# Softmax weights scaled in place, turned plainly, and routing moved beside the out-projection

## The reference, cut to what matters

```
def sink_softmax(s, sink):            # s: (..., queries, keys)
    col = broadcast(sink)             # one more column, dropped after
    return softmax(concat([col, s], -1), -1)[..., 1:]
...
p = sink_softmax(concat([s_loc, s_ctx], -1), sink)
o = einsum(p[..., :span], v) + einsum(p[..., span:], v_ctx)
...
g_val, g_idx = top_k(g_logit, 1)      # group
e_val, e_idx = top_k(e_logit[group], 2)
gates = p_group * softmax(e_val)
```

## Time and profile before

| | |
|---|---|
| median of 3 runs | 3037.66 us (3034.0 to 3044.69) |
| the profiled execution | 3045.0 us, span 3043.2 us |
| PE busy in the span | 2741.7 us (90%) |
| DVE, ACT, POOL busy | 1069.0, 459.5, 316.7 us |
| mean granted clock of TensorE | 0.945 of full speed |
| data read from HBM | 743.04 MB |
| attention, layers 0 and 1 | 1278 to 1386, 2232 to 2322 us |
| out-projection, layers 0 and 1 | 1386 to 1478, 2323 to 2382 us |
| routing to the first expert product | to 1530, to 2428 us |
| experts' loops | to about 2072, to about 2997 us |

### The profile page before, as it was taken

One profiled execution on the slowest core, in us unless ns is written; L12 is line 12 of the kernel. 1 busy time (PEld: TensorE's weight loads), 2 busy tenths in 40 slices (PEclk: granted clock), 3 DMA queues, 4 the chain that ended last, 5 costly groups with the idle time before them and its releaser, 6 DMA issues.

```text
span 3043.2 us, 33073 instructions
## 1 busy us (share of the span) xinstructions
PE 2741.7 (90%) x11436; PEld 1249.1 (41%) x11436; DVE 1069.0 (35%) x2093; ACT 459.5 (15%) x874; POOL 316.7 (10%) x445
## 2 busy tenths in 40 slices
PE   7999999999998999999689898986999699999863
PEld 3444444444444446565433232322555433333321
DVE  4999960320003032364631111115544521111104
ACT  3111121100101010451101000002142100101000
POOL 0101112000000000000122111110000121122110
PEclk9999999999998999999799999997989699999986
DMA  6656341212220211001579999995201699999983
GB/s 226 218 189 198 111 181 57 100 56 82 83 83 1 94 56 56 28 1 71 207 284 393 395 393 393 391 341 223 100 1 51 222 358 394 385 347 337 361 326 134
DMA packets 272217, 603.12 MB, mean 198 GB/s; under 512 B 18436, under 2 KB 43332, under 8 KB 272000
## 3 DMA queue, kind: packets, MB, share of 16 engines
q1 hardware_dynamic: 256864, 580.70, 52.2%
q0 software_dynamic: 15264, 21.24, 2.0%
HBM read 743.04 MB, written 29.20 MB: 254 GB/s over the span
## 4 chain that ended last, share of the span: by engine, by line
PE 74%; SPq 10%; DMA 7%; DVE 5%; issue 2%; ACT 2%; POOL 0%; POOLq 0%; DVEq 0%; ACTq 0%
PE psum L1408 13%; PE psum L1020 11%; PE psum L1107 11%; PE psum L1242 9%; SPq L655 9%; PE psum L1078 7%; DMA arena<-in_w 5%; PE psum L1430 5%; PE psum L1346 5%; PE psum L1289 3%; PE psum L1278 2%; PE psum L1005 1%; PE psum L1128 1%; PE psum L1395 1%; PE psum L1301 1%
## 5 line engine op out<-in xcount | busy, mean ns | idle before, releaser
L1408 PE MATMUL psum<-arena 128*64 128x512 f32 x2656 | 639.5, 626 | 89.0 <-DMA arena<-in_w 87.3
L1408 PEld LDWEIGHTS psum<-arena 128*64 128x64 f32 x2656 | 191.9, 143 | 415.9 <-issue 410.7
L1020 PE MATMUL psum<-arena 128*128 128x512 f32 x768 | 341.2, 600 | 2.6 <-ACTq L752 2.6
L1107 PE MATMUL psum<-arena 128*128 128x512 f32 x768 | 329.9, 593 | 0.8 <-ACT arena L731 0.8
L1430 PE MATMUL psum<-arena 128*64 128x512 f32 x1328 | 303.1, 600 | 0.8 <-issue 0.8
L1507 DVE SCALAR_TENSOR_TENSOR arena<-arena 128x512 f32<-128x512 f32 x451 | 300.1, 745 | 0.0
L1242 PE MATMUL psum<-arena 128*128 128x512 f32 (+1 forms) x800 | 288.4, 520 | 5.4 <-ACT arena L818 5.4
L1078 PE MATMUL psum<-arena 128*128 128x512 f32 x512 | 224.4, 602 | 5.2 <-POOL arena L2205 4.4
L1107 PEld LDWEIGHTS psum<-arena 128*128 128x128 f32 x768 | 146.1, 190 | 184.0 <-issue 183.0
L1020 PEld LDWEIGHTS psum<-arena 128*128 128x128 f32 x768 | 143.7, 191 | 176.9 <-issue 174.0
L1242 PEld LDWEIGHTS psum<-arena 128*128 128x128 f32 x800 | 151.7, 192 | 128.8 <-issue 113.4
(11 more groups left out here) (294 smaller groups left out, 2055.1 us busy)
## 6 DMA issues: line engine op xcount, KB each, us to landing
arena<-in_w SPq DMA_DIRECT2D x261, 2048.0 KB, 19.0
arena<-in_w_ada SPq DMA_DIRECT2D x48, 1024.0 KB, 5.2
arena<-in_conv_w_in SPq DMA_DIRECT2D x24, 1024.0 KB
arena<-in_ret_w_in SPq DMA_DIRECT2D x12, 2048.0 KB, 7.9
arena<-in_w_in SPq DMA_DIRECT2D x8, 2048.0 KB, 9.3
arena<-moe_out SPq DMA_DIRECT2D x10, 1024.0 KB, 10.2
arena<-in_conv_w_out SPq DMA_DIRECT2D x4, 2048.0 KB, 11.9
arena<-in_ret_w_out SPq DMA_DIRECT2D x4, 2048.0 KB, 7.8
```

Source lines behind the costliest of these rows:

```text
L1020: m = pe.matmul(bank(b + c), w[:, k, c * P:(c + 1) * P], c_hT[:, k, :], start=(k == 0), stop=(k == KD - 1))
L1107: m = pe.matmul(bank(4 * (n % 2) + j), l_, r_, start=(k == 0), stop=(k == KD - 1))
L1408: m = pe.matmul(bank(2 * s)[part], m_xsT[s][:, at:at + SB], m_w[s][j][:, k, :], start=(k == 0), stop=(k == KD - 1))
```

## The change

In the attention the diagonals are gone. `weights` multiplies the exponentials themselves, in place in `b_sb` (128 rows by 256, 512 or 640 keys per head), by the reciprocal, and `turn` is a plain transpose against the identity. `sink_shift`, `sink_exp` and `weights` are split in two halves of four heads; on DVE the first half of `weights(i+1)` stands after the chunk before the last of tile i, the second after its last.

In the out-projection, from the third tile on, PE turns tile t-1 between the two halves of product t, and the logits of tile t-1 follow product t directly (before: t-2). On DVE the copy and the rows of tile i-1 stand between the two half sums of tile i. The routing operations become a function `route(t0, t1)`, called after the norm of tile i for the tiles whose logits are due (tiles 0 and 1 together, then one each), and once more for the last two tiles where the whole routing stood.

```diff
 def turn(i, c, kv):
...
-                        m = pe.matmul(bank(4 + kv, P, hh * P), b_sb[i % 2][:, 4 * kv + hh, c * P:(c + 1) * P],
-                                      b_dg[i % 2][:, 4 * kv + hh, :], start=True, stop=True)
+                        m = pe.transpose(bank(4 + kv, P, hh * P), b_sb[i % 2][:, 4 * kv + hh, c * P:(c + 1) * P], ident)
...
                     for hf in range(2):
+                        if hf == 1 and t >= 2:
+                            mod_transposes(2 * l + 1, t - 1)
...
-                    if t >= 1:
-                        mod_transposes(2 * l + 1, t - 1)
+                    if t == 1:
+                        mod_transposes(2 * l + 1, 0)
+                    if t == 2:
+                        pe.wait_ge(sem("wr"), past("wr", l) + 16)
+                        logits(0)
                     if t >= 2:
-                        pe.wait_ge(sem("wr"), past("wr", l) + 16)
-                        logits(t - 2)
-                logits(nt - 2)
+                        logits(t - 1)
                 mod_transposes(2 * l + 1, nt - 1)
                 logits(nt - 1)
...
                 for i_ in range(nt):
-                    stats_of(i_)
                     if free:
+                        first(i_, tiles[i_], 0)
                         if i_ >= 1:
                             mod_copy(mod_q, i_ - 1)
-                        norm(i_)
                         if 1 <= i_ < nt - 1:
                             rows(i_ - 1)
+                        first(i_, tiles[i_], 1)
+                        stats_of(i_)
+                        norm(i_)
+                        if 2 <= i_ < nt - 1:
+                            route(i_ - 1 if i_ > 2 else 0, i_)
                         continue
...
+                def weights(i, half):
+
+                    o = 100 + 40 * (i % 2) + 4 * half
+                    W = P * len(att_keys(queries[i]))
+                    rs, esk, rinv = (stats[:, o + 8 * j:o + 8 * j + 4] for j in (2, 3, 4))
+                    dve.wait_ge(sem("at_e"), past("at_e", l) + (AH + 2) * i + 5 * (half + 1))
                     link(dve.tensor_tensor(rs, rs, esk, ALU.add))
                     link(dve.reciprocal(rinv, rs))
-                    for h in range(AH):
-                        dve.tensor_scalar(b_dg[i % 2][:, h, :], ident, rinv[:, h:h + 1], None, ALU.mult)\
-                            .then_inc(sem("at_p"), 1)
+                    for hh in range(4):
+                        p = b_sb[i % 2][:, 4 * half + hh, 0:W]
+                        dve.tensor_scalar(p, p, rinv[:, hh:hh + 1], None, ALU.mult).then_inc(sem("at_p"), 1)
...
-                        if more and nk > 2 and c in (1, 2):
-                            masked(i + 1, c + 1)
-                        if more and c == min(nk, 3) - 1:
-                            sink_shift(i + 1)
-                        if more and c == min(nk, 4) - 1:
-                            weights(i + 1)
+                            sink_shift(i + 1, c)
+                        elif more and c == 1:
+                            sink_shift(i + 1, 0)
+                            masked(i + 1, 2)
+                        elif more and c == 2:
+                            masked(i + 1, 3)
+                            sink_shift(i + 1, 1)
+                        if more and c == max(nk - 2, 0):
+                            weights(i + 1, 0)
+                        if more and c == nk - 1:
+                            weights(i + 1, 1)
...
+                def route(t0, t1):
+
+                    n, r = t1 - t0, slice(t0, t1)
+                    dve.wait_ge(sem("lg_mm"), past("lg_mm", l) + t1)
...
+                finish_rows(2 * l, tiles, add_product, 2 * l + 1,
+                            lambda: dve.wait_ge(sem("ob_mm"), past("ob_mm", l) + 2 * nt), route)
+                route(nt - 2, nt)
```

More of the change, by code:

```diff
@@ L907, in attended @@
                                            o[:, :, h_, :], ACT.Copy).then_inc(sem("at_o"), 1)
-                for pair in range(4):
-                    exps(0, pair)
-                sink_exp(0)
+                for half in range(2):
+                    exps(0, 2 * half)
+                    exps(0, 2 * half + 1)
+                    sink_exp(0, half)
                 mixed_copied(nt - 1)
@@ L924, in _ @@
                             exps(i + 1, 2 * c + 1)
-                        if more and c == min(nk, 4) - 1:
-                            sink_exp(i + 1)
+                            sink_exp(i + 1, c)
+                        elif more and c in (1, 3):
+                            sink_exp(i + 1, c // 2)
                 attended(nt - 1)
@@ L1653, in _, with finish_rows @@
             r_gate(RH - 1)
-            def finish_rows(q, tiles, first, mod_q, free=None):
+            def finish_rows(q, tiles, first, mod_q, free=None, route=None):
                 nt = len(tiles)
                 def stats_of(i_):
-                    first(i_, tiles[i_])
                     for hf in range(2):
@@ L1897, in _ @@
                 masked(0, 3)
-                sink_shift(0)
-                weights(0)
+                sink_shift(0, 1)
+                weights(0, 0)
+                weights(0, 1)
                 for i in range(nt):
@@ L1966, in _, with first_of @@
                 iota = mem(TAB + T_I, 120)
-                def first_of(dst, idx, vals, top, width):
-                    it = iota[:, 0:width].unsqueeze(1).to_broadcast([P, nt, width])
-                    link(dve.tensor_tensor(dst, vals, over(top, nt, width), ALU.is_equal))
+                def first_of(dst, idx, vals, top, n, width):
+                    it = iota[:, 0:width].unsqueeze(1).to_broadcast([P, n, width])
+                    link(dve.tensor_tensor(dst, vals, over(top, n, width), ALU.is_equal))
@@ L1979, in _ @@
-                link(dve.tensor_reduce(gmax, lg[:, :, 0:NG], AX.X, ALU.max))
-                dve.tensor_tensor(ge, lg[:, :, 0:NG], over(gmax, nt, NG), ALU.subtract).then_inc(sem("rt_dve"), 1)
-                first_of(goh, gi, lg[:, :, 0:NG], gmax, NG)
-                link(dve.tensor_scalar(gc, goh, -1.0, BIG, ALU.add, ALU.mult))
-                for t in range(nt):
-                    link(dve.tensor_tensor(el[:, t, :].rearrange("p (g e) -> p g e", g=NG),
-                                           lg[:, t, NG:NG + E].rearrange("p (g e) -> p g e", g=NG),
-                                           gc[:, t, :].unsqueeze(2).to_broadcast([P, NG, EPG]), ALU.add))
@@ L1996, in _ @@
[L1996 to L1997 removed]
+                    link(dve.tensor_tensor(dst, dst, over(idx, n, width), ALU.is_equal))
+                def route(t0, t1):
+                    n, r = t1 - t0, slice(t0, t1)
+                    dve.wait_ge(sem("lg_mm"), past("lg_mm", l) + t1)
+                    rb = mem(SMALL + V_RB + (NG + E) * l, NG + E).unsqueeze(1).to_broadcast([P, n, NG + E])
+                    logit = bank(6, (NG + E) * n, (NG + E) * t0).rearrange("p (t e) -> p t e", t=n)
+                    group = lg[:, r, 0:NG]
+                    link(dve.tensor_tensor(lg[:, r, :], logit, rb, ALU.add))
+                    link(dve.tensor_reduce(gmax[:, r], group, AX.X, ALU.max))
+                    last_ge = dve.tensor_tensor(ge[:, r, :], group, over(gmax[:, r], n, NG), ALU.subtract)
+                    if t1 == nt:
+                        last_ge.then_inc(sem("rt_dve"), 1)
+                    first_of(goh[:, r, :], gi[:, r], group, gmax[:, r], n, NG)
+                    link(dve.tensor_scalar(gc[:, r, :], goh[:, r, :], -1.0, BIG, ALU.add, ALU.mult))
+                    for t in range(t0, t1):
+                        link(dve.tensor_tensor(el[:, t, :].rearrange("p (g e) -> p g e", g=NG),
+                                               lg[:, t, NG:NG + E].rearrange("p (g e) -> p g e", g=NG),
+                                               gc[:, t, :].unsqueeze(2).to_broadcast([P, NG, EPG]), ALU.add))
+                    link(dve.tensor_reduce(m1[:, r], el[:, r, :], AX.X, ALU.max))
+                    first_of(oh1[:, r, :], i1[:, r], el[:, r, :], m1[:, r], n, E)
+                    link(dve.scalar_tensor_tensor(out=el[:, r, :], in0=oh1[:, r, :], scalar=-3 * BIG, in1=el[:, r, :],
+                                                  op0=ALU.mult, op1=ALU.add))
+                    link(dve.tensor_reduce(m2[:, r], el[:, r, :], AX.X, ALU.max))
+                    first_of(oh2[:, r, :], i2[:, r], el[:, r, :], m2[:, r], n, E)
+                    last_ed = dve.tensor_tensor(ed[:, r], m2[:, r], m1[:, r], ALU.subtract)
+                    if t1 == nt:
+                        last_ed.then_inc(sem("rt_dve"), 1)
+                    link(dve.tensor_tensor(M[:, r, :], oh1[:, r, :], oh2[:, r, :], ALU.add))
+                    if t0 == 0:
+                        link(dve.memset(before[:, 0, :], 0.0))
+                    for t in range(t0, min(t1, nt - 1)):
+                        link(dve.tensor_tensor(before[:, t + 1, :], before[:, t, :], M[:, t, :], ALU.add))
```

65 lines of the change are left out of this document (23 added, 42 removed).

## The result

The changed kernel took 3022.8 us in the median of 7 runs (3021.3 to 3027.6), the kernel before 3042.6 beside it (3034.0 to 3044.7). The ratio is 0.9948 (95% interval 0.9934 to 0.9961): 12 to 20 us faster, where 34.5 were forecast and 3003 us with them. Its profiled execution has a span of 3019.9 us, that of the kernel before 3043.2.

A forecast was written before the change was run, and what follows sets the result against it. PE bounds the attention (busy 98.9 of 108 and 83.4 of 90 us); DVE has room. Attention 34, less 4 for the clock, plus 4.5 from the tails: 34.5 us off the median of 3037.66 gives 3003, range 2989 to 3020.

The forecast's parts named there:

- The larger one, plus 0.7 for the hand-over: Attention tile: larger of PE's 14.9 and DVE's 15.5 us, plus 0.7, makes 16.2 instead of 20.7, a gain of 4.5.
- The rival of growing hand-overs: Attention: DVE becomes the limit and its hand-overs grow; gain 15 us in all, 3023 us, chance 0.18.
- its price of 0.72 for the scaling: Attention on DVE: scaling 640 elements in place costs 0.72 us instead of 0.55, a tile 1.4 us more.
- The turn at 0.44 us: Attention on PE: a plain-transpose call takes 0.44 us instead of 0.99, saving at least 0.55 on each of 80 calls.
- Clock, 4 us: Attention on PE: two more half-clock stretches of 7 us, each costing about 2 us, 4 us taken off.
- Nothing of PE waits: Out-projection: routing on DVE fits beside the products and transposes between halves get their norm in time; cost nothing.
- The tail: After the last out-projection product: 2.6 us of steps move ahead, gather issued 5.6 us earlier in layer 0, 3.9 in layer 1.
- The gather, 2.5 us given back: First expert gather in each layer: runs beside the first experts' weights on the DMA engines, giving back 2.5 us.
- +4.5: Out-projection tails of both layers after the gather's loss: 3.1 and 1.4 us left, 4.5 in all, bounds 0 and 9.5.
- The range: Whole kernel: measured time expected between 2989 and 3020 us.
- transposes between halves with an idle time ahead of them: Out-projection on PE: listed among the signs that would show the forecast wrong; no size given.
- rival A: Attention: DVE becomes the limit, hand-overs grow; gain 15 us, 3023 us, chance 0.18; sign: scaling 640 elements well over 0.55 us.

The follow-up runs named there:

- comb1: Changed kernel; ACT makes four- and five-key tiles' last second copy, two-key tiles scale next first half later, tile 0's logits between halves: 3003.2 us, ratio 0.9890.
- w_late: Changed kernel with the scaling of the next tile's first half moved behind the last chunk's copy on DVE: one run, 3008.3 us.
- act_copy: Changed kernel with the second copy of a tile's last chunk moved from DVE to ACT: 3013.3 us, ratio 0.9916.
- no_scale: Changed kernel without the scaling of the weights, so softmax isn't normalised: tiles 81.4 and 59.5 us, whole time not comparable.
- comb2: comb1, but four- and five-key tiles scale the next tile's first half between third chunk's copy and last masked scores: 3000.5 us, ratio 0.9884.
- sp_hold: Changed kernel with the second expert stream's first weights requested only after the first gather has landed: one run, 3039.2 us.
- route_only: Kernel before with only the out-projection and routing edits, attention as before: 3039.4 us, ratio 1.0006.
- tr3: Changed kernel with tile 1's transposes kept behind tile 2's product, between halves only from tile 3's product on: one run, 3018.3 us.

## Why the prediction was wrong

With two profiles of each kernel the account closes. Means, before less after: tiles 7.2 us in layer 0 and 9.3 in layer 1; first out-product to first expert product +0.2 and -3.2; the last loop 2.1; starts, loop of layer 0 and what lies ahead -1.1. Sum 14.5, against 15.8 by the ratio. That PE bounded the attention and that the change is faster by more than 0.3% was right; the size was not. (The 3003 us also stood on a median of 3037.66 for the kernel before, which was 3042.6 beside the change; that alone would have made it 3008.)

- **"The larger one, plus 0.7 for the hand-over"**: the step that failed. The time that it gave can be had: the tile takes 16.48 us in comb1 for 16.2, and start and tiles together 87.6 for the 108.2 of before where 18.2 less were forecast, 75.9 for 90.4 where 15.7 less were. But an engine is only as busy as its sum if the work that others wait for isn't behind work that nobody needs yet. DVE scaled the next tile ahead of the copy that PE's last values wait for, and it waited for ACT ahead of masked scores. The tiles got 7.2 and 9.3 us. That this order costs PE its time is shown in layer 0 by w_late, where nothing but the order changed; in layer 1 w_late gave 1.6 us, all of it clock, and more is shown only together with the copy moved to ACT (act_copy, comb1). The rival of growing hand-overs (15 us in all, 3023, chance 0.18) had this place and the time nearly right, though not its price of 0.72 for the scaling: that was 0.55.
- **The turn at 0.44 us**: mis-sized. It became 0.51 a call in pairs and 0.59 alone; the ten of the tile went from 10.11 to 5.45 us, so a call saves 0.47, not 0.55. With the scores, which grew beside it, PE's sum of the tile is 16.4 in no_scale, not 14.9. The forecast had the limit on DVE (15.5 to 14.9); measured, PE's sum is the larger (16.2 to 13.9 in comb1), so that the 16.2 us of the tile came so near is luck in part. I had taken the lowest price at hand for calls that alternate with scores and values.
- **Clock, 4 us**: too small. No row showed a stretch of 7 us that costs 2; those seen behind waits last some 3.4 us and cost 1.2 to 1.7. With the same instructions and the same form of both starts, PE is busy over the tiles 78.3 and 58.0 us in after and 72.8 and 56.0 in comb2: 7.5 us. It comes with DVE's waits, not with the transposes: a clock of 0.92 and 0.93 in after, 0.98 and 0.95 in comb2.
- **"Nothing of PE waits" in the out-projection**: failed at tile 1. I took the norm's 4.3 us from the tail, where nothing stands ahead of it (it took 4.8 there). In the loop DVE's queue has the copy of tile 0 (1.36) and its scaled rows (1.21) ahead of the second half sum, and that sum took 2.42 beside POOL: the norm was done at 1416.0, 9.8 us behind the product's end at 1406.2. And tile 1 has no logits behind it, so it was due at 7.8. Without the 1.7 us lost beside POOL some 0.3 of the wait of 2.0 would be left (an estimate from these rows); neither delay was tested apart.
- **The tail**: right in layer 0. From the last product to the rank matmul pass 18.85 us (1476.55 to 1495.40); forecast were 27.1 less 2.6 and 5.6, 18.9. But that product ended 98.0 us into the stage instead of the forecast 94.1, by the wait and the half clock: of 5.6 us earlier, 1.75 were left; in layer 1 of 3.9, 0.6: there the wait took 2.0, and the tail 19.7 us for a forecast of 18.7, with the last transposes at half clock (1.97 us for 1.09).
- **The gather, 2.5 us given back**: right, from the gather to its reader 3.72 us became 5.74 in layer 0 and 2.6 became 5.6 in layer 1, with the DMA engines busy 0.26 of the first stretch and 0.89 of the second in layer 0, and sp_hold shows its cause. With so little won ahead of it, it turned the routing half into a loss of 3 us up to the experts in layer 1, which a last loop 2.1 us shorter nearly covered: +4.5 became about 0 (route_only).
- **The range** ended at 3020; the median was 3 us beyond. It rested on sums of busy time, not on the order of the queues.

The stated sign of the wrong case, "transposes between halves with an idle time ahead of them", was there; the sign for rival A (scaling well over 0.55 us) was not, and A's outcome came by another way.

## What to carry to other kernels

When work moves from the busiest engine to one with room, sums of busy time tell what can be reached; the in-order queue of the receiving engine tells what will be. List for each of its instructions who waits for it, and put none that nobody needs yet, or that waits itself, ahead of one that the critical engine will soon need. And read single stages against the same marks in two executions of each kernel before believing a difference of a few microseconds.

## What the runs showed of the hardware

- An fp32 transpose of 128 x 128 has no single price at full clock: 0.109 us each in a run of eight, 0.13 in a pair of calls, 0.15 in a lone call of four between other products (against about 0.25 for the full fp32 matmul).
- PE's clock at the start of a stage is no property of the kernel: layer 1's attention started near full clock (0.91 to 1.00 up to the first turn) in 7 of the 16 profiles and at 0.51 or 0.52 in the others. With the same instructions both forms occur, 4.1 us apart for the kernel before and 4.5 for the changed one.
- The same wait of 2.0 us, ahead of tile 1's transposes, was followed at once by a stretch at half clock in 5 of 16 out-projections, 1.2 to 1.7 us lost, and not in the others; tr3 had such a stretch once with no wait ahead of it. What decides it stays open.
- A DVE sum of two SBUF operands (128x512) took 2.42 us instead of 0.69 beside a POOL sum of 2.34 us.
